# One decoder step on one core: all pages of the key and value cache issued by SyncE's queue

## What is computed

```python
k_past = cache_k[j][page_table].reshape(db, past_len, KV_HEADS, HEAD_DIM)
v_past = cache_v[j][page_table].reshape(db, past_len, KV_HEADS, HEAD_DIM)
...
logits = jnp.einsum('bqhd,bqhsjd->bqhsj', qi, kg) * scale   # own block and the best 3 of 8
p = jax.nn.softmax(logits, axis=-1)
return jnp.einsum('bqhsj,bqhsjd->bqhd', p, vg)
```

## Time and profile before

| | |
|---|---|
| time, median of 3 runs | 1921.53 us (1921.21 to 1923.94) |
| the profiled execution, its time | 1925.23 us |
| the profiled execution, its span | 1923.0 us |
| TensorE busy | 1779.1 us, 93% |
| VectorE busy | 1293.0 us, 67% |
| ScalarE busy | 968.4 us, 50% |
| moved | 521.85 MB, mean 271 GB/s |
| mean granted clock | 0.951 |

### The profile page before, as it was taken

How to read it: one execution, slowest core, us unless ns; L and a number is a source line. 1 busy time by engine, 2 the same in 40 slices (tenths; PEclk the granted TensorE clock), 3 DMA queues, 4 the chain that set the end, 5 groups by cost and what they waited for, 6 DMA issues and landing times.

```text
span 1923.0 us, 26967 instructions
## 1 busy us (share of the span) xinstructions
PE 1779.1 (93%) x9794; PEld 1483.7 (77%) x9794; DVE 1293.0 (67%) x1399; ACT 968.4 (50%) x908; POOL 53.3 (3%) x82
## 2 busy tenths in 40 slices
PE   5999988899999973896999999999999999999996
PEld 4888886899997731365888888888888888888885
DVE  5864573555543241014888888988889888888885
ACT  3442230444431030002777777776777777777773
POOL 1240000000000000000000000000000000000000
PEclk9998798999999996885999999999999999999998
DMA  7322123355546699972899999999999999999991
GB/s 291 110 80 103 48 118 154 138 190 177 178 157 238 201 325 386 346 300 89 317 363 384 346 370 362 345 382 350 365 365 334 387 352 362 371 348 358 357 351 57
DMA packets 98893, 521.85 MB, mean 271 GB/s; under 512 B 11066, under 2 KB 11259, under 8 KB 46067
## 3 DMA queue, kind: packets, MB, share of 16 engines
q1 hardware_dynamic: 82592, 482.72, 66.8%
q10 hardware_dynamic: 13970, 25.46, 3.7%
q0 software_dynamic: 2240, 12.49, 1.8%
HBM read 512.30 MB, written 8.33 MB: 271 GB/s over the span
## 4 chain that ended last, share of the span: by engine, by line
PE 78%; issue 9%; DVE 7%; ACT 2%; ACTq 2%; DMA 1%; SPq 1%; POOLq 0%; POOL 0%; DVEq 0%
PE bank L994 14%; PE bank L996 14%; PE bank L995 14%; PE bank L503 6%; PE bank L504 5%; PE bank L505 5%; PE bank L744 3%; PE bank L810 3%; PE bank L911 1%; PE bank L615 1%; PE bank L988 1%; PE bank L1033 1%; ACTq L408 1%; PE bank L660 1%; DVE ring L1625 1%
## 5 line engine op out<-in xcount | busy, mean ns | idle before, releaser
L1829 DVE TENSOR_TENSOR w_lo<-raw_w,w_hi 128x2048 fp32r<-128x2048 f32 x336 | 768.8, 2290 | 120.7 <-ACT w_hi L1276 116.4
L1276 ACT ACTIVATE w_hi<-raw_w 128x2048 fp32r<-128x2048 f32 x336 | 644.8, 1920 | 362.4 <-PE bank L996 273.5
L994 PE MATMUL bank<-w_hi,xe_hi 128*128 128x512 f32 x896 | 364.9, 407 | 1.5 <-DVE xe_lo L1890 1.5
L996 PE MATMUL bank<-w_hi,xe_lo 128*128 128x512 f32 x896 | 350.1, 391 | 0.0
L995 PE MATMUL bank<-w_lo,xe_hi 128*128 128x512 f32 x896 | 349.5, 390 | 0.0
L504 PE MATMUL bank<-fh_lo,w_hi 128*128 128x264 f32 x704 | 202.3, 287 | 0.0
L996 PEld LDWEIGHTS bank<-w_hi,xe_lo 128*128 128x128 f32 x896 | 168.6, 188 | 36.0
L994 PEld LDWEIGHTS bank<-w_hi,xe_hi 128*128 128x128 f32 x896 | 168.7, 188 | 35.8 <-issue 1.8
L995 PEld LDWEIGHTS bank<-w_lo,xe_hi 128*128 128x128 f32 x896 | 168.8, 188 | 33.8
L994 PE MATMUL bank<-w_hi,aT_hi 128*128 128x512 f32 x448 | 176.7, 394 | 0.0
L996 PE MATMUL bank<-w_hi,aT_lo 128*128 128x512 f32 x448 | 174.7, 390 | 0.0
(11 more groups left out here) (340 smaller groups left out, 2204.7 us busy)
## 6 DMA issues: line engine op xcount, KB each, us to landing
raw_w<-in_moe SPq DMA_DIRECT2D x336, 1024.0 KB, 5.6
raw_w<-in_ffn_w SPq DMA_DIRECT2D x42, 1024.0 KB, 4.8
ring<-in_k_pages SPq DMA_DIRECT2D x96, 256.0 KB, 3.5
raw_w<-in_gdn_in SPq DMA_DIRECT2D x16, 1024.0 KB, 5.2
ring<-in_v_pages SPq DMA_DIRECT2D x64, 256.0 KB, 11.7
ring<-in_v_pages ACTq DMA_DIRECT2D x64, 256.0 KB, 11.6
ring<-in_att_in SPq DMA_DIRECT2D x4, 2048.0 KB, 7.7
ring<-in_k_pages ACTq DMA_DIRECT2D x32, 256.0 KB, 7.7
```

What stands on the lines that cost most here:

```text
L994: mm(out, hi, move_hi, start=first, stop=False)
L996: return mm(out, lo, move_hi, start=False, stop=last)
L1276: A(w_hi[:, p % SPLIT, :], raw_w[:, p % RAW, :], ACT.Copy).then_inc(split_hi, 1)
L1829: V.tensor_tensor(w_lo[:, p % SPLIT, :], raw_w[:, p % RAW, :], w_hi[:, p % SPLIT, :].bitcast(F32), ALU.subtract).then_inc(split_lo, 1)
```

## The change

ScalarE no longer issues cached pages. Its three calls of `load_pages` are taken out, and SP issues all eight pages of every chunk, in the same order of chunks. `C_BOTH` is gone. Slots, semaphores, their values and all arithmetic stay as they were.

```diff
-        C_BOTH = C_K + SLOTS
...
             for n in range(C_K, C_AOUT):
-                load_pages(sp, n, range(0, PPC) if n < C_BOTH else range(0, PPC // 2))
+                load_pages(sp, n, range(PPC))
...
                 if i < H:
                     p_exp(i)
-                if i >= 1:
-                    load_pages(act, C_BOTH + i - 1, range(PPC // 2, PPC))
-            for n in range(C_BOTH + H + 1, C_V + SLOTS):
-                load_pages(act, n, range(PPC // 2, PPC))
             act.wait_ge(bias_done, 1)
...
                     .then_inc(probT_sb, 1)
-            for n in range(C_V + SLOTS, C_AOUT):
-                load_pages(act, n, range(PPC // 2, PPC))
             def split_piece(v, p, first=False):
```

## The result

The changed kernel takes 2001.69 us (median, 1996.62 to 2003.26) against 1921.37 us (1918.53 to 1923.94) of the kernel before: a ratio of 1.0414 with a 95% interval of 1.0390 to 1.0438, 80 us slower. The prediction was 2001, between 1991 and 2011.

A forecast was written before the change was run, and what follows sets the result against it. The prediction took SP's issue rate as the bound, 1.117 us a page against 0.68 to move it. A projection 77.3 us later plus 2.1 of clock gave 79.4 on the median 1921.53: 2001 us, range 1991 to 2011.

The forecast's parts named there:

- Pace: SP's page issues from the first shared chunk on: 1.117 us a page, bounded by 1.113 and 1.128.
- SP never waits for key or value products: SP's shared pages: no wait for free slots; the 15.2 us wait for the first value chunk goes.
- Start of the value products: TensorE's value products, after keys, biases and exponentials: start at 781.6 us.
- Landing of the last page: End of the page stage: the last page lands 3.0 us after its issue, where it took 12.5 before.
- From the last chunk's products to the projection: End of the stage on TensorE: 6.8 us at the low clock, where it was 5.96.
- Start of the projection: First product of the output projection: at 910.2 us instead of 832.90, +77.3 us.
- Clock in the projection: The projection's first 2 to 6 us run at the low clock: +2.1 us, bounds 0 and 4.
- Expert weights and the loads of the projection: Loads behind SP's pages: projection's first 2.1 MB just in time (up to 3 us late), expert weights covered.
- ScalarE's gain hidden: Exponentials no longer wait 18.1 us for ScalarE's page issues, but this buys nothing, since value products follow SP's pages.
- rival 1: Page stage: transfer stays the bound, SP feeds it alone and exponentials come 18.1 us earlier: 1903 us; chance 2%.

The follow-up runs named there:

- late exponentials: The changed kernel with 40 more exponentials of the same tiles ahead of the eight that are used: 2000.2 us.
- fixed pages: The changed kernel with each page read from a fixed place in the cache, without the lookup in the table: 1917.9 us.
- rebalanced: The kernel before, with ScalarE's shares from C_V+4 on cut to 3 of 8 pages and moved behind the copies of the turned probabilities: 1916.3 us.

## Why the prediction held, step by step

The bound was named rightly: SP's issue rate. Each step of the sum has its line.

- Pace: 1.117 us taken. From the first shared page, which falls 84.0 us after SP's first (84.6 before), to the last are 896.32 - 681.51 = 214.8 us, 1.125 each; predicted 213.4.
- SP never waits for key or value products: 0.2 us, as said.
- Start of the value products at 781.6 predicted, 777.5 measured; with the stage 4.9 us early, 782.4.
- Landing of the last page: 3.0 taken, 3.5 measured; most value pages take 2.9 (median of the 128).
- From the last chunk's products to the projection 6.8 us at the low clock: 906.66 - 899.89 = 6.77.
- Start of the projection: +77.3 predicted, +78.6 measured. The 1.3 is made up, to 0.1, of the pace (+1.4), of the time from the last page's issue to its products (3.6 us for 3.0) and of the first shared page, which falls 0.6 us sooner after the stage's first product.
- Clock in the projection: +2.1 predicted, +2.5 measured. The clock was 0.50 until almost 912, 5 us into the projection, near the far end of the 2 to 6 that I had given. That this term came out so well is partly luck. I had taken two places where the low level lasted 9 to 13 us of work, as if it were a property of the pause; one chunk earlier in the changed kernel it ended at about 894.7, 4.4 us after the products began (890.31, above):

```profile
888.00:890.00 2.00, 0.00 (x0) 0.00 (x0) 0.00 (x0) 0.00 (x0) 0.00 (x0) 0.50 0.84 237
890.00:894.00 4.00, 3.69 (x17) 0.72 (x17) 0.00 (x0) 0.00 (x0) 0.00 (x0) 0.50 0.85 243
894.00:895.00 1.00, 1.00 (x7) 1.00 (x7) 0.00 (x0) 0.00 (x0) 0.00 (x0) 0.65 0.71 244
```

TensorE worked without a gap there, while behind the last chunk it waits twice, 0.81 and 0.45 us. Had the clock risen after 4.4 us there too, this term would have been nothing. So "at the low clock" was right for most value products, not for the stage: there the mean clock from 720 to 900 us is 0.61.

- Expert weights and the loads of the projection were covered: no wait for them, and the rest of the program is the same within 1.0 us.
- ScalarE's gain hidden: shown by the late exponentials, for 14 us of the 18.1.

One thing beside the sum was wrong. I called ScalarE's 18.1 us before the exponentials time on the path and priced rival 1 with them, at 1903 us. The kernel that realizes rival 1, with fixed pages, takes 1917.9, and the rebalanced one, whose exponentials start 20.4 us sooner, 1916.3. What I had not looked at: SP did stand 15.2 us before C_V+8, but the engines worked on through most of it on pages already queued. The trace of before shows them run dry for 3 to 4 us only:

```profile
770.00:775.00 5.00, 4.71 (x23) 4.52 (x22) 0.25 (x1) 1.19 (x2) 0.00 (x0) 0.50 1.05 386
775.00:777.00 2.00, 1.93 (x12) 0.68 (x16) 0.02 (x1) 0.00 (x0) 0.00 (x0) 0.50 0.47 176
777.00:779.00 2.00, 2.00 (x13) 0.45 (x8) 0.00 (x0) 0.00 (x0) 0.00 (x0) 0.50 0.09 35
779.00:780.00 1.00, 1.00 (x12) 0.29 (x8) 0.00 (x0) 0.00 (x0) 0.00 (x0) 0.65 0.00 0
```

The share (last but one) falls only behind 775. Where the transfer was the bound, an earlier start of its consumer was worth the time in which the engines were empty, and little more: 6 us of 20.

The rule in the Trainium skill that I set against the forecast ("DMA: Bandwidth & Descriptors", "Issuing engines are not separate DMA queues") holds here in its mechanism and not in its "usually small": the second queue is worth nothing more than issue time, as the fixed pages show at 387 GB/s on one queue, but at 1.12 us to issue and 0.68 to move the issue time is the larger of the two.

## What to carry to other kernels

Compare, for each queue and each part of a stage, the distance between two issues with the time the bytes need; here a transfer of 256 KB whose address comes from a table costs its queue 1.12 us and the DMA engines 0.68. A second issuer is worth the issue time of the pages that it takes off the pacing queue, as long as the engines have room (35.4 us for 32 pages); and a stretch that leaves the engines idle is not made up for by a later one that fills them. Before pricing a wait that goes away, see how much work is still queued behind it.

## What the runs showed that I had not expected

- ScalarE's page issues between the prompt heads cost nothing. Key products follow each other at 5.31 us in the changed kernel as well (693.06, 698.36, 703.67), though ScalarE issues nothing there.
- Issuing slows down when the engines are full: with constant addresses the median DMA instruction takes 552 ns for value pages, 327 at the least and up to 1581, and so brings SP to the 0.68 us of the transfer by itself.
- A loaded number that is never used costs its full 0.55 us. SP runs its instructions one by one: in the trace of the changed kernel each starts 28 ns or more after the end of the one before (45 in the median), which makes the 0.27 us of gaps in a page. Their order hardly helps (1.082 for 1.121 us a page).
